# Branch B's score maps, four at a time on TensorE's four groups of 32 rows

## What is computed

```python
h = rmsnorm(x, norm_g[l]);  p = split(h @ w_in[l])
o_a = mla(...)          # branch A: latent attention, 4 heads, up projections w_uq, w_ukv
o_b = diff_attn(...)    # branch B: 4 heads, two score maps for each
o_c = dsa(...)          # branch C: attention to the top 128 keys by an indexer
o_d = short_conv(...)   # branch D
x = x + concat(o_a*silu(gate), o_b*..., o_c*..., o_d*...) @ w_out[l]
# branch B, for a block of 128 queries, d = 32, keys up to the block's own chunk of 64:
logits = einsum('bqhmd,bkhmd->bhmqk', q, k) * 32**-0.5 + bias     # m = 0, 1
p = masked_softmax(logits)
o = (p[:, :, 0] - lam * p[:, :, 1]) @ v
```

## Time and profile before

| what | value |
|---|---|
| median of 3 runs | 1786.4 us |
| span of the profiled execution | 1785.4 us |
| TensorE busy in the span | 1776.4 us (99%) |
| VectorE, ScalarE, GpSimd busy | 1062.3, 750.5, 407.3 us |
| branch B's steps, first layer | 74.4 to 164.0 us |
| branch B's steps, second layer | 384.4 to 474.0 us |

### The profile page before, as it was taken

The page is one execution under the profiler, slowest core; times in us unless marked ns, Lnnn a source line. Parts: engine busy times, 40 slices in busy tenths (PEclk is TensorE's granted clock), DMA queues, the critical chain, the costliest instruction groups (busy, mean ns, idle before and its releaser), DMA issues.

```text
span 1785.4 us, 25187 instructions
## 1 busy us (share of the span) xinstructions
PE 1776.4 (99%) x9274; PEld 1437.2 (80%) x9274; DVE 1062.3 (59%) x2106; ACT 750.5 (42%) x1386; POOL 407.3 (23%) x248
## 2 busy tenths in 40 slices
PE   9999999999999999999999999999999999999998
PEld 7767778776777888888888878879888888888887
DVE  5888777588877665445433445555756654555333
ACT  6464654446454533223222455545444322232222
POOL 4544553455354310000000232220200200000000
PEclk9999999999999999999999999999999999999999
DMA  5422222322212343333333422323321333333332
GB/s 188 125 81 70 60 59 85 97 81 83 67 53 60 96 138 102 95 94 94 106 106 104 150 60 83 95 72 107 95 73 55 92 101 94 94 94 101 99 106 94
DMA packets 49765, 165.53 MB, mean 93 GB/s; under 512 B 5640, under 2 KB 6152, under 8 KB 49672
## 3 DMA queue, kind: packets, MB, share of 16 engines
q1 hardware_dynamic: 48376, 161.47, 30.2%
q10 hardware_dynamic: 1296, 2.84, 0.4%
HBM read 162.12 MB, written 2.17 MB: 92 GB/s over the span
## 4 chain that ended last, share of the span: by engine, by line
PE 97%; DVE 1%; ACT 1%; issue 0%; POOL 0%; DVEq 0%; POOLq 0%
PE proj L1013 78%; PE turned L1302 2%; PE o L1326 2%; PE score L1276 2%; PE turned L1530 1%; PE proj L1460 1%; PE o L1556 1%; PE score L1521 1%; PE proj L1453 1%; PE score L1285 1%; PE o L1652 1%; PE turned L979 1%; PE score L1641 1%; PE score L1163 0%; PE proj L991 0%; PE turned L998 0%
## 5 line engine op out<-in xcount | busy, mean ns | idle before, releaser
L1013 PE MATMUL proj<-hhi,whi 128*128 128x512 f32 x1456 | 580.2, 399 | 0.6 <-DVE tanh L2285 0.3
L1013 PE MATMUL proj<-hhi,wlo 128*128 128x512 f32 x1456 | 568.1, 390 | 0.0
L1013 PE MATMUL proj<-hlo,whi 128*128 128x512 f32 x1456 | 567.3, 390 | 0.0
L1736 ACT ACTIVATE whi<-ring 128x1024 fp32r<-128x1024 f32 x279 | 295.2, 1058 | 622.7 <-PE proj L1013 614.4
L2201 DVE TENSOR_TENSOR wlo<-ring,whi 128x1024 fp32r<-128x1024 f32 x199 | 243.1, 1222 | 164.8 <-ACT whi L1736 164.5
L1013 PEld LDWEIGHTS proj<-hhi,whi 128*128 128x128 f32 x1456 | 274.3, 188 | 59.4 <-issue 6.6
L1013 PEld LDWEIGHTS proj<-hhi,wlo 128*128 128x128 f32 x1456 | 273.4, 188 | 58.8
L1013 PEld LDWEIGHTS proj<-hlo,whi 128*128 128x128 f32 x1456 | 274.0, 188 | 52.8
L759 POOL TENSOR_TENSOR wlo<-ring,whi 128x1024 fp32r<-128x1024 f32 x80 | 194.7, 2435 | 372.6 <-ACT whi L1736 372.0
L771 POOL TENSOR_TENSOR prob<-prob 128x512 f32<-128x512 f32 x36 | 56.6, 1574 | 873.9 <-ACT prob L1732 873.9
L1762 ACT ACTIVATE prob<-prob,negmax 128x256 f32<-128x256 f32 (+3 forms) x208 | 114.4, 552 | 65.5 <-DVE negmax L2274 64.1
(11 more groups left out here) (334 smaller groups left out, 2426.1 us busy)
## 6 DMA issues: line engine op xcount, KB each, us to landing
ring<-wstream SPq DMA_DIRECT2D x287, 512.0 KB, 3.6
arena<-lines SPq DMA_DIRECT2D x28, 256.0 KB, 5.5
arena<-x ACTq DMA_DIRECT2D x4, 512.0 KB, 5.9
out<-arena SPq DMA_DIRECT2D x8, 256.0 KB, 2.9
arena<-mem SPq DMA_DIRECT2D x1, 1024.0 KB, 9.4
ring<-wstream ACTq DMA_DIRECT2D x2, 256.0 KB, 7.3
arena<-hot SPq DMA_DIRECT2D x2, 80.0 KB
par<-params ACTq DMA_DIRECT2D x2, 74.0 KB, 1.9
```

The lines of the kernel that those rows point to most:

```text
L1013: mm = pe.matmul(b, rounded(w), rounded(rhs(v, k)), start=(first and n == 0 and p == 0), stop=(last and n == len(blocks) - 1 and p == 2))
L1736: act.activation(rounded(dst), src, ACT.Copy, scale=scale).then_inc(ready, 1)
```

## The change

In the steps 2, 4, ..., 14 `scores` issues the maps of two steps, s and s + 1, that is both heads of the pair: 3 passes of 4 matmuls on the four groups of 32 rows. The banks are score[0], score[1], turned[1], and opsum[1] (opsum[0] in steps 12 and 14). In the odd steps 3 to 15 it issues nothing. Steps 0 and 1, A and C are as before. The softmax and all that follows stay one head a step; VectorE reads the maps of an odd step from the third and fourth bank. turned[1] is taken, so B's transposes all go to turned[0], and UK, UV, VN0 and VN1 move from opsum[1] to turned[0], with waits both ways: the filler waits until the transposes of its step have been copied out (`turned_there`), and the transposes of the next step wait until the filler's result has been copied out. The costs of the planner and the order of the fillers change with it.

```diff
-FILLERS = ("BQ1", "VN0", "BK1", "VT1", "UK0", "UQ0", "UK1", "UQ1", "UQ2", "UV0", "UQ3", "UV1", "GT0", "VN1", "GT1", "GT2", "GT3",
-           "DB0", "VT2", "DB1", "VN2", "VT3", "SQ0", "SK0", "VN3", "SQ1", "SK1", "SS0", "DC0", "SR0", "DC1", "SR1",
+FILLERS = ("BQ1", "VN0", "BK1", "VT1", "UK0", "UQ0", "UQ1", "UK1", "UQ2", "UV0", "UQ3", "UV1", "GT0", "GT1", "VN1", "GT2", "GT3",
+           "DB0", "VT2", "DB1", "VT3", "VN2", "SQ0", "SK0", "VN3", "SQ1", "SK1", "SS0", "DC0", "SR0", "DC1", "SR1",
...
+def quad_step(s):
+
+    return 2 <= s < B_STEPS and s % 2 == 0
...
-    if s < STEPS:
+    if quad_step(s):
+        blocks += 0.2 + 0.2 * (step_qb(s) + 1)
+    elif s < 2 or B_STEPS <= s < STEPS:
         blocks += (0.25 if s < B_STEPS or s >= C_STEP else 0.44) * (step_qb(s) + 1)
...
+IN_TURNS = [name for name in FILLERS if name[:2] in ("UK", "UV") or name in ("VN0", "VN1")]
+def quad_out(s):
+
+    return 1 if s < B_STEPS - 4 else 0
+def used_before(s, kinds):
+
+    return sum(END[name] < s for name in IN_TURNS if name[:2] in kinds)
...
-        V_BANK = (opsum[1], opsum[1], opsum[0], opsum[1])
+        V_BANK = (turned[0], turned[0], opsum[0], opsum[1])
+        def turn_bank(g):
+            return turned[0] if g < B_STEPS else turned[g % 2]
+        def quad_bank(s, u):
+            return (score[0], score[1], turned[1], opsum[quad_out(s)])[u]
+        def score_bank(s, b):
+            return quad_bank(s - 1, 2 + b) if 2 <= s < B_STEPS and s % 2 else score[b]
...
+                def turned_there(name):
+
+                    if END[name] >= 2:
+                        pe.wait_ge(turn_out, L * LAYER_GR + (END[name] - 1))
...
+                    if n == 2:
+                        pe.wait_ge(min_ready, L * LAYER_SM + 2 * B_STEPS)
...
-                    w, b = raw_slot("UK"), opsum[1]
+                    w, b = raw_slot("UK"), turned[0]
+                    turned_there(f"UK{pair}")
...
-                    w, b = raw_slot("UV"), opsum[1]
+                    w, b = raw_slot("UV"), turned[0]
+                    turned_there(f"UV{half}")
...
+                    if 2 <= s < B_STEPS and s % 2:
+                        return
...
+                    if quad_step(s):
+                        if s == 2:
+                            pe.wait_ge(latent_ready, L * 3 + 3)
+                        if quad_out(s) == 0 and quad_out(s - 2) == 1:
+                            pe.wait_ge(o_free[0], L * 3 + 1)
+                        for p, (q_part, k_part) in enumerate(((bq_hi, bk_hi), (bq_hi, bk_lo), (bq_lo, bk_hi))):
+                            for u in range(4):
+                                branch, pair, qb, h, m = UNITS[2 * s + u]
+                                W, r = width(qb), HD * h + 32 * m
+                                mm = pe.matmul(quad_bank(s, u)[:, 0:W], rounded(q_part[r:r + 32, pair, qb * P:(qb + 1) * P]),
+                                               rounded(k_part[r:r + 32, pair, 0:W]), start=(p == 0), stop=(p == 2))
+                                if p == 2:
+                                    mm.then_inc(score_done, 1)
+                        return
...
+                    for kinds, copied in ((("VN",), v_copied), (("UK", "UV"), up_out)):
+                        if used_before(s + 2, kinds) > (used_before(s + 1, kinds) if s else 0):
+                            pe.wait_ge(copied, L * 4 + used_before(s + 2, kinds))
...
-                        if g >= 2:
-                            pe.wait_ge(turn_out, L * LAYER_GR + (g - 1))
+                        if g >= 1:
+                            pe.wait_ge(turn_out, L * LAYER_GR + (g if g <= B_STEPS else g - 1))
```

More of the change, by code:

```diff
@@ L270 @@
 ENDED = [[name for name in FILLERS if END[name] == s] for s in range(FILL_STEPS)]
+IN_TURNS = [name for name in FILLERS if name[:2] in ("UK", "UV") or name in ("VN0", "VN1")]
 O_STEP = (10, 18, 22, 26, 32, 34)
+def quad_out(s):
+    return 1 if s < B_STEPS - 4 else 0
+def used_before(s, kinds):
+    return sum(END[name] < s for name in IN_TURNS if name[:2] in kinds)
+assert max(END[name] for name in IN_TURNS) < B_STEPS and END["VN2"] >= B_STEPS - 1
+assert quad_out(O_STEP[0] - 1) == 1 and quad_out(O_STEP[0] + 2) == 0
 SQUARE_STEP = O_STEP[1] + 1
@@ L686, in _ @@
                     sp.wait_ge(job_done, layer_job(L, JOBS[SLOT_JOB[i]]) + 1)
+                    if i == SLOT_OF["UK"]:
+                        sp.wait_ge(up_done, L * 4 + 2)
                     if i == SLOT_OF["UV"]:
@@ L1109, in raw_slot @@
                     return ring[:, i % RING, :]
+                def turned_there(name):
+                    if END[name] >= 2:
+                        pe.wait_ge(turn_out, L * LAYER_GR + (END[name] - 1))
                 def turn_v(n):
                     wait_out(pe, L, f"VT{n}")
+                    if n == 0:
+                        pe.wait_ge(latent_ready, L * 3 + 3)
                     if n == 1:
                         pe.wait_ge(up_out, L * 4 + 4)
+                    if n < 2:
+                        turned_there(f"VN{n}")
                     if n >= 2:
                         pe.wait_ge(o_free[n - 2], L * 3 + 1)
+                    if n == 2:
+                        pe.wait_ge(min_ready, L * LAYER_SM + 2 * B_STEPS)
                     for t in range(NT):
@@ L1294, in turn @@
                     qb = step_qb(s)
-                    if s == 0:
-                        pe.wait_ge(latent_ready, L * 3 + 3)
+                    for kinds, copied in ((("VN",), v_copied), (("UK", "UV"), up_out)):
+                        if used_before(s + 2, kinds) > (used_before(s + 1, kinds) if s else 0):
+                            pe.wait_ge(copied, L * 4 + used_before(s + 2, kinds))
                     pe.wait_ge(scaled_ready, L * LAYER_SM + (2 * s + 2))
                     for n, g in enumerate(step_groups(s)):
-                        if g >= 2:
-                            pe.wait_ge(turn_out, L * LAYER_GR + (g - 1))
+                        if g >= 1:
+                            pe.wait_ge(turn_out, L * LAYER_GR + (g if g <= B_STEPS else g - 1))
                         for kb in range(qb + 1):
-                            mm = pe.transpose(turned[g % 2][:, kb * P:(kb + 1) * P],
+                            mm = pe.transpose(turn_bank(g)[:, kb * P:(kb + 1) * P],
                                               prob[:, (2 * s + n) % 4, kb * P:(kb + 1) * P], ident[:, :])
@@ L1897, in copy_up_k @@
                     act.wait_ge(up_done, L * 4 + (pair + 1))
-                    act.activation(kA[0:HD, 2 * pair, :], opsum[1][0:HD, :], ACT.Copy)
-                    act.activation(kA[0:HD, 2 * pair + 1, :], opsum[1][HD:P, :], ACT.Copy).then_inc(up_out, 1)
+                    act.activation(kA[0:HD, 2 * pair, :], turned[0][0:HD, :], ACT.Copy)
+                    act.activation(kA[0:HD, 2 * pair + 1, :], turned[0][HD:P, :], ACT.Copy).then_inc(up_out, 1)
                 def copy_up_v(half):
                     act.wait_ge(up_done, L * 4 + (half + 3))
-                    act.activation(vA[:, 2 * half:2 * half + 2, :], opsum[1][:, :].rearrange("p (t c) -> p t c", c=256), ACT.Copy)\
+                    act.activation(vA[:, 2 * half:2 * half + 2, :], turned[0][:, :].rearrange("p (t c) -> p t c", c=256), ACT.Copy)\
                         .then_inc(up_out, 1)
@@ L1942, in _ @@
                                 act.wait_ge(pv_done, L * LAYER_GR + (g - 3))
-                            act.activation(pT[:, g % 4, 0:W], turned[g % 2][:, 0:W], ACT.Copy).then_inc(turn_out, 1)
+                            act.activation(pT[:, g % 4, 0:W], turn_bank(g)[:, 0:W], ACT.Copy).then_inc(turn_out, 1)
                     if s < STEPS:
@@ L2446, in row_mins @@
                     for b in range(2):
-                        row_min((2 * s + b) % 4, width(step_qb(s)), score[b], bias_of(2 * s + b))
+                        row_min((2 * s + b) % 4, width(step_qb(s)), score_bank(s, b), bias_of(2 * s + b))
                 def row_scales(s):
```

## The result

The changed kernel takes 1794.43 us (median of 5 runs, 1794.03 to 1797.44), the kernel before 1785.95 in the same comparison: ratio 1.0052, interval 1.004 to 1.0064. It is 8.5 us slower, where 1782.2 was forecast and the range ended at 1786.5. The forecast was wrong, and in its sign.

The account below looks back on a forecast made before the run. TensorE, working 99% of the span, was taken as the bound. Per layer 5.35 - 2.3 - 0.75 - 0.2 = 2.1 us, both 4.2, so 1786.4 - 4.2 = 1782.2 us; range 1778.5 to 1786.5.

Parts of the forecast that it names:

- What it removes: TensorE, branch B's odd steps 3 to 15: seven pairs' bodies, 4.79 us, and leads, 0.56; 5.35 us saved a layer.
- The quads at nothing: Branch B's even steps: six more matmuls each add no time, since the widest stream sets the time.
- Rival 2: Quads' wide streams disturb each other (0 to 6.5 us), GpSimd delays DB0 or one clock dip remains; together chance 0.24.
- the 2 us of the estimate: Quads: by the skill's 3.07 times for four row groups at 512 columns, about 2 us of the saving would go.
- The wait of step 5: TensorE waits before step 5's transposes for ScalarE's copy of UK1: 2.3 us a layer, bounds 1.3 and 3.6.
- of step 7: TensorE waits before step 7's transposes for the copy of UV1: 0.75 us a layer, up to 1.5.
- GpSimd at DB0: GpSimd's queue of low parts and rotary jobs holds up DB0: 0.2 us a layer, bounds 0 and 1.
- only moves fillers: Planner's new costs shift fillers between steps; on a TensorE that is never idle, this costs nothing.
- TensorE's clock at nothing: Today's 1.7 us dip may go, step 5's wait may bring one a layer: nothing summed, range -1.7 to +3.4.
- rival 3: Clock falls at each wait of steps 5 and 7, both layers: 6.8 us against 4.2 gained, 1789.0; chance 0.08.
- What lies around the span: Median run 1786.4 against profiled span 1785.4: 1.0 us lies outside the span and stays.

Follow-up runs that it names:

- Experiments 6 and 7: Changed kernel with VN3 in step 20, UK and UV in opsum[1], quads only in steps 8 to 14: 1781.08 us; with step 2's quad too: 1780.17 us.
- Experiment 5: On top of experiment 1, ScalarE copies UK out before UQ when both end in a step: 1781.78 us, ratio 0.9977.
- experiment 1: Changed kernel with VN3 behind SQ1 in the list of fillers, dealt to step 20 instead of 18: 1784.51 us, ratio 0.9993.
- experiment 2: Kernel before, pairs and own banks kept, with only the changed kernel's order of fillers and planner costs, UK's slot load held: 1796.27 us, ratio 1.0055.
- experiment 3: Changed kernel, VN3 unmoved, GpSimd's low part after SQ0 held until VectorE has scaled step 17's maps: 1787.97 us, ratio 1.0009.
- experiment 8: On top of the faster kernel of Experiments 6 and 7, GpSimd's four rotary jobs each a step later (8 to 11): 1782.26 us.

## Why the prediction was wrong

**What it removes: right.** Seven pairs a layer at 5.35 us; with the waits counted from start to start the profiled execution adds up with it. Experiments 6 and 7 leave out four and five of the seven, 5.9 and 7.8 us by these prices; less the waits that came up, 1.3 and 2.0 us, that is 4.6 and 5.8, and 4.8 and 5.9 were measured.

**The quads at nothing: right.** 0.90, 0.56, 0.73 and 0.48 us at widths 512, 256, 384 and 128 against 0.89, 0.55, 0.72 and 0.47 of the pairs. Rival 2's disturbed streams don't show: four full widths took 131.24 to 132.13, 0.89 us. The 3.07 times of the Trainium skill ("TensorE: Matmul & The Clock Gate", the part on packing small matmuls), which spoke for them, are a speedup over no packing; no row here has one group alone, but going from two groups to four cost 0.00 to 0.01 us, so the 2 us of the estimate were not lost.

**The wait of step 5: right**, 2.64 and 2.31 us for 2.3 forecast, **of step 7: right**, 0.69 for 0.75. Experiment 5 shows that the cause is the one named, UQ1 ahead of UK1 in ScalarE's queue.

**GpSimd at DB0:** 0.38 for 0.2, the right place, inside its bounds.

**The planner "only moves fillers ... On an engine that is never idle that costs nothing": the step that failed.** It treats a filler as TensorE's time alone. VN3 also needs opsum[1], which VectorE frees in its step 18, O_STEP[1]; it lay in step 19 and moved to 18, beyond step 16, where my table of moved fillers stopped. (The sentence below that table is wrong too: by the planner's lists both kernels have done the same only from the end of step 22 on.) I had looked at UV0, VN1 and VN2, and never asked for VN3. And a slot's low part moved with its projection onto VectorE's scaling, which made the copy 1.8 us later still. Together 6.3 us of waits. Experiments 1, 2 and 3 show it from three sides.

**TensorE's clock at nothing: mis-sized.** I set a dip that may come against one that may go. In the profiled execution four came (8.5 us lost) and one went (1.7): +6.8 us. Filling the waits gives 4.0 of it back in the median. This was rival 3's mechanism, but only in part at its places: the clock fell behind both waits of step 5 and both of VN3, 2.3 to 3.2 us long, and behind neither wait of step 7.

**What lies around the span** was taken as 1.0 us; for the profiled run of after it is 1797.44 - 1795.6 = 1.8. That has no part in the miss.

Not settled: why the same wait of 3.16 us cost 1.7 and 3.4 us of clock in the two layers of after, and 5.1 and 1.7 in those of experiment 2.

## What to carry to other kernels

When a planner is given new costs, every job that it moves is a change of its own: list for each one the bank or buffer that it needs, who frees that and in which step, and compare the two before counting its time as neutral. Two jobs that share one bank in turns need work between them that needs neither; put the copy that others wait for first in its engine's queue. A wait of two or three microseconds on TensorE can cost as much again in the clock behind it (0 to 5.1 us behind the waits of 2.3 to 3.2 us here), so a saving that is paid for with idle time may be none: experiment 1 leaves out 10.7 us of matmuls, idles for 6.4 and is not faster than before.

## What the runs showed of the hardware

VectorE's TENSOR_SCALAR in SBUF did not share time with GpSimd's TENSOR_TENSOR, it took until that had ended: 3.92 us for two that take 0.88, beside 2.36 and 1.47 us of GpSimd's. The Trainium skill has the rule ("SBUF — State Buffer", section on who interferes with whom): VectorE has a second port pair that it shares with GpSimd and uses in some modes, which a tensor_scalar can enter; whoever issues first holds the pair for its whole instruction, and the other is blocked. The trace agrees, also in who came first (178.94 against 179.10, then 181.27 against 181.51), though it doesn't show the mode; experiment 3 takes the collision away. The kernel before has the same thing at other steps, where TensorE doesn't wait for it: two scalings of 128x256 took 1.43 us at 183.38, beside GpSimd's 1.26 from 183.13, and take 0.62 in after.

TensorE went to 1.2 GHz in or behind nine of the ten idle times of 2.3 to 3.2 us in the profiles of after and experiments 1 to 3, for 3.4 us in seven cases, 6.8 in one and 10.2 in one; the tenth, 2.65 us in the first layer of experiment 1, had no dip. It did not fall behind 1.29 to 1.38 us (experiments 3 and 5) or 0.7. Ten or thirteen matmuls of no use in the wait kept it at 2.4 GHz. The dip of the earlier trace rows, without idle time, came in the first layer of before and of experiment 1 and in the second of experiment 8, and in no other profile.
